# A hybrid encoder layer on one core: VectorE's rows taken in twos, half of the one-hots on ScalarE, shorter norms, and another order of GELUs and gate loads

## What is computed

```python
q = (xt @ w_pq).reshape(T, 8, 256)
s1 = einsum('thd,nd->thn', q[..., :128], sub_keys1)     # 128 keys each
s2 = einsum('thd,nd->thn', q[..., 128:], sub_keys2)
v1, i1 = top_k(s1, 16); v2, i2 = top_k(s2, 16)
cand_s = (v1[..., :, None] + v2[..., None, :])          # 256 pairs
cand_i = (i1[..., :, None] * 128 + i2[..., None, :])
top_s, pos = top_k(cand_s, 16)
idx, gate = cand_i at pos, softmax(top_s)               # 8 heads x 16 experts per token
act = gelu(einsum('thkd,td->thk', peer_u[idx], x)) * gate
out = einsum('thk,thkd->td', act, peer_v[idx])
x = layer_norm(ALPHA * x + out)
```

## Time and profile before

| | us |
|---|---|
| median of 3 runs (lowest, highest) | 3692.41 (3690.04, 3693.42) |
| the profiled execution, whole | 3718.29 |
| its span in the trace | 3716.4 |
| PE busy in the span | 3221.2 (87%) |
| DVE busy | 2060.8 (55%) |
| POOL busy | 782.7 (21%) |
| ACT busy | 374.4 (10%) |

### The profile page before, as it was taken

One profiled execution on the slowest core, in us unless ns is written; L12 is line 12 of the kernel. 1 busy time (PEld: TensorE's weight loads), 2 busy tenths in 40 slices (PEclk: granted clock), 3 DMA queues, 4 the chain that ended last, 5 costly groups with the idle time before them and its releaser, 6 DMA issues.

```text
span 3716.4 us, 27290 instructions
## 1 busy us (share of the span) xinstructions
PE 3221.2 (87%) x10446; PEld 1944.9 (52%) x10446; DVE 2060.8 (55%) x2868; ACT 374.4 (10%) x653; POOL 782.7 (21%) x546
## 2 busy tenths in 40 slices
PE   7998988899997597995555799959899997999995
PEld 4443433334445376774445444658544885448742
DVE  5356023232646767776777767555555554556564
ACT  1233012220102101110111000000000000000000
POOL 0000000000011102223222222343333433233230
PEclk9999998999998798997777899979999998999998
DMA  6221210037885567997777898998989999899992
GB/s 237 68 76 59 90 55 31 23 141 267 304 306 214 213 247 276 373 373 290 294 287 285 338 386 336 397 404 353 405 354 404 392 389 383 348 420 401 390 399 98
DMA packets 160817, 1031.76 MB, mean 278 GB/s; under 512 B 16448, under 2 KB 32960, under 8 KB 43328
## 3 DMA queue, kind: packets, MB, share of 16 engines
q0 software_dynamic: 75520, 547.39, 36.7%
q1 hardware_dynamic: 85184, 482.83, 33.8%
HBM read 1009.18 MB, written 20.97 MB: 277 GB/s over the span
## 4 chain that ended last, share of the span: by engine, by line
PE 50%; DVE 20%; DMA 20%; issue 5%; POOL 2%; ACT 1%; SPq 0%; DVEq 0%; ACTq 0%
PE ps L1032 15%; DMA arena<-peer_u,arena 12%; PE ps L1005 10%; PE ps L646 9%; DVE arena L1656 5%; PE ps L804 3%; DMA arena<-peer_ut 3%; DVE arena L1645 2%; PE ps L894 2%; DMA arena<-peer_v,arena 2%; POOL arena L579 2%; DVE arena L1683 2%; DMA arena<-peer_vt 2%; DVE arena L1585 1%; DVE arena L1582 1%
## 5 line engine op out<-in xcount | busy, mean ns | idle before, releaser
L1005 PE MATMUL ps<-arena 128*128 128x256 f32 x4096 | 896.3, 382 | 52.5 <-DMA arena<-peer_ut 52.5
L1032 PE MATMUL ps<-arena 128*128 128x512 f32 x2048 | 890.1, 598 | 49.5 <-DMA arena<-peer_vt 26.5
L1645 DVE CUSTOM_DVE_ANT_0 arena<-arena 128x2048 f32<-128x2048 f32 x256 | 586.3, 2290 | 559.3 <-DMA arena<-peer_u,arena 558.9
L1005 PEld LDWEIGHTS ps<-arena 128*128 128x128 f32 x4096 | 783.1, 192 | 162.4 <-issue 54.0
L1032 PEld LDWEIGHTS ps<-arena 128*128 128x128 f32 x2048 | 393.2, 192 | 544.2 <-issue 519.8
L579 POOL DMA_INDIRECT arena<-peer_v,arena x256 | 398.9, 1558 | 1126.6 <-DVE arena L1656 1096.5
L1656 DVE SCALAR_TENSOR_TENSOR arena<-arena 128x2048 f32<-128x2048 f32 x256 | 601.4, 2349 | 49.1 <-DMA arena<-peer_v,arena 44.2
L568 POOL DMA_INDIRECT arena<-peer_u,arena x256 | 368.2, 1438 | 925.6 <-DVE arena L1645 679.0
L646 PE MATMUL ps<-arena 128*128 128x512 f32 x832 | 363.3, 599 | 12.0 <-ACT arena L1111 11.0
L646 PEld LDWEIGHTS ps<-arena 128*128 128x128 f32 x832 | 160.0, 193 | 213.7 <-issue 213.7
L1069 ACT ACTIVATE arena<-ps 128x512 f32<-128x512 f32 (+4 forms) x247 | 146.7, 611 | 1030.1 <-PE ps L1017 224.7
(11 more groups left out here) (174 smaller groups left out, 1962.2 us busy)
## 6 DMA issues: line engine op xcount, KB each, us to landing
arena<-peer_ut SPq DMA_DIRECT2D x128, 1024.0 KB, 9.6
arena<-peer_vt SPq DMA_DIRECT2D x128, 1024.0 KB, 9.1
arena<-w_row SPq DMA_DIRECT2D x52, 1024.0 KB, 4.9
arena<-w_mix SPq DMA_DIRECT2D x48, 1024.0 KB, 4.8
arena<-w_once SPq DMA_DIRECT2D x76, 512.0 KB, 3.5
arena<-w_feat SPq DMA_DIRECT2D x20, 1024.0 KB, 4.8
dense_gates<-arena SPq DMA_DIRECT2D x8, 2048.0 KB, 6.7
arena<-dense_gates SPq DMA_DIRECT2D x16, 1024.0 KB, 18.8
```

The costliest lines, as they stand in the source:

```text
L1005: last = pe.matmul(ps[:, (e // 2) % 4, (e % 2) * DT:(e % 2 + 1) * DT], w[:, kt * P:(kt + 1) * P], XTD[:, kt * DT:(kt + 1) * DT], start=(kt ...
L1032: last = pe.matmul(bank(4 + (c % 2) * 2 + tb), G[:, t * DT + tb * P:t * DT + (tb + 1) * P], w[:, i * 512:(i + 1) * 512], start=(t == 0), s ...
L1645: dve.tensor_tensor_reduce(UB[e], UB[e], xrow(b), 1.0, 0.0, ALU.mult, ALU.add, DOT[r // 4 % 2][:, r % 4:r % 4 + 1]).then_inc(u_free, 1)
```

## The change

- **Rows.** `row_step` becomes `row(k)`: dot of row k+4, then add of row k. `some_rows(n)` does the next n rows. Before the tail VectorE takes rows in twos, mostly between the two halves of a routing, which is split into `best_keys` and `best_pairs`, and after it. 90 rows come before V0 instead of 84; in the tail they are spread in halves of a step (`half_pos`). The second V buffer opens at row 13 instead of 9.
- **One-hots.** VectorE makes only the gated one, with four `tensor_scalar` of 128x128 for each step; ScalarE makes the other with four Abs of 128x128 (the distance of the iota from the number) and one Relu of 128x512 (1 - distance). TensorE waits for both. They come in 16 groups of four steps before U tiles 17 to 32, with two rows of VectorE's within each group.
- **Routings of block 1.** Their products move to after U tiles 2, 5, 8, 11, the transposition to after tile 15. Two of the four routings come before V0, the other two at positions 8 and 15.
- **Norms.** Two passes in place of three. In the last dense group the statistics of blocks 2 and 3 are taken column group by column group, block 1's norm stands ahead of the last `add_dense`, and the last two blocks share one reciprocal square root.
- **ScalarE.** `gelu_rows` and `gate_exps` stand elsewhere between the evictions; `d_turned("x2T")` comes ahead of the GELU it followed.
- **Gates.** In groups 1 to 3 `load_gates` comes later in SyncE's queue, and `weigh` comes at positions 12 and 18 of a U phase and early in the V phase instead of after every eighth position.

```diff
-PQ_AFTER = [3, 7, 11, 15]
-TURN_AFTER = 21
-ONEHOT_BEFORE = [24 + 2 * k for k in range(DT // TG)]
+PQ_AFTER = [2, 5, 8, 11]
+TURN_AFTER = 15
+ONEHOT_FROM = 17
-ROWS_BEFORE = 21
-ROUTE_POS = [2, 12, 19, 26]
+HALVES_BEFORE = 45
+ROUTE_POS = {8: 2, 15: 3}
-V1_FROM = 9
+V1_FROM = 13
 (SyncE)
-                    for i in range(TILES[g] // 8):
-                        q = FIRST[g] // 8 + i
-                        if g and q + 2 < NK // 8 and p == start + 8 * i + 7 + SLOTS:
-                            load_gates(q + 2)
+                    q, n = FIRST[g] // 8, TILES[g] // 8
+                    if g and p == start + TILES[g] - 4:
+                        load_gates(q + 2)
+                    if g and n > 3 and p == start + TILES[g] - 2:
+                        load_gates(q + 3)
+                    if 0 < g < 3 and p == start + TILES[g] + 20:
+                        load_gates(q + n)
+                        load_gates(q + n + 1)
 (TensorE)
-                    pe.wait_ge(oh_ready, n + 1)
+                    pe.wait_ge(first_hot, n + 1)
+                    pe.wait_ge(second_hot, n + 1)
 (ScalarE)
+            def second_one_hots(n):
+                if n >= 2:
+                    act.wait_ge(oh_mm, n - 1)
+                hot = OH[n % 2][:, 4 * NK:8 * NK]
+                for k in range(4):
+                    t = DT + 4 * n + k
+                    last = act.activation(hot[:, k * NK:(k + 1) * NK], IOTA, ACT.Abs, bias=TB[:, t:t + 1])
+                last.then_inc(hot_dist, 1)
+                act.wait_ge(hot_dist, n + 1)
+                act.activation(hot, hot, ACT.Relu, bias=ONES[:, 0:1], scale=-1.0).then_inc(second_hot, 1)
+            for n in range(DT // 4):
+                if n % 8 == 0 and n:
+                    gelu_rows()
+                second_one_hots(n)
+                if n:
+                    stage_gates(n - 1)
+                if n % 8 == 5:
+                    gelu_dense(0, t)
+                    t += 2
 (VectorE)
-                link(dve.tensor_scalar(dst, src, MV[:, 0:1], RSTD, ALU.subtract, ALU.mult))
-                link(dve.tensor_tensor(dst, dst, gain, ALU.mult))
-                return dve.tensor_tensor(dst, dst, bias, ALU.add)
+                link(dve.scalar_tensor_tensor(out=dst, in0=src, scalar=MV[:, 0:1], in1=gain, op0=ALU.subtract, op1=ALU.mult))
+                return dve.scalar_tensor_tensor(out=dst, in0=dst, scalar=RSTD, in1=bias, op0=ALU.mult, op1=ALU.add)
+            def row(k):
+                j, part = divmod(k, 4)
+                if part == 0:
+                    dve.wait_ge(gel_done, j + 1)
...
+                if j + 1 < RSTEPS:
+                    dot(k + 4)
+                if part == 0:
+                    dve.wait_ge(act_done, j + 1)
+                add_row(k)
+            def first_one_hots(n):
+                if n >= 2:
+                    dve.wait_ge(oh_mm, n - 1)
+                for k in range(4):
+                    t = 4 * n + k
+                    last = dve.tensor_scalar(OH[n % 2][:, k * NK:(k + 1) * NK], IOTA, TB[:, t:t + 1],
+                                             TB[:, 2 * DT + t:2 * DT + t + 1], ALU.is_equal, ALU.mult)
+                last.then_inc(first_hot, 1)
+            def d_route(n, between):
+                b, c = 2 + n % 2, n // 2 - 2
+                best_keys(n, f"d.key{c}.{n % 2}")
+                some_rows(between)
+                best_pairs(b, c)
...
                 for k, b in enumerate((3, 1)):
                     add_mix(b, c, (c % 2) * 2 + k, f"mix31.{c}")
-                if c == 0:
-                    row_step(0)
-                if c == 1:
-                    gates(1, 0, 1)
-                if c == 2:
-                    row_step(1)
+                if c < 2:
+                    some_rows(4)
             first_norm(3, "mix3.3")
...
-            for n in range(8, 12):
-                route(n, 2 + n % 2, n // 2 - 2, f"d.key{n // 2 - 2}.{n % 2}")
-                if n < 11:
-                    row_step(n)
-                gates(n, 2 + n % 2, n // 2 - 2)
-            row_step(11)
+            for n in range(6, 12):
+                d_route(n, 2)
+                some_rows(2)
+                d_gates(n)
             dve.wait_ge(tb_ev, 1)
-            for k in range(DT // TG):
-                row_step(12 + k)
-                for n in range(8 * k, 8 * k + 8):
-                    one_hot(n)
-            row_step(12 + DT // TG)
+            for n in range(DT // 4):
+                first_one_hots(n)
+                if n % 4 == 1:
+                    some_rows(2)
+            best_keys(12, "b1.key0")
+            best_pairs(1, 0)
+            some_rows(2)
+            gates(12, 1, 0)
+            best_keys(13, "b1.key1")
+            best_pairs(1, 1)
...
+                    if g == 3 and c == 3:
+                        rows_until(POSITIONS)
+                        dve.wait_ge(v_free, 2 * HK)
+                        norm(ACC1, ACC1, GAIN3_G, GAIN3_B, dve_tick).then_inc(y_ready, 1)
                     add_dense(g, c)
+                    if g == 3:
+                        last = last_stats(c)
...
+            rsqrt(RSTD3, var, NEWTON3)
+            for tb in range(DB):
+                xr = xrow(2 + tb)
+                link(dve.scalar_tensor_tensor(out=xr, in0=xr, scalar=MV3[:, 2 * tb:2 * tb + 1], in1=GAIN3_G,
+                                              op0=ALU.subtract, op1=ALU.mult))
+                dve.scalar_tensor_tensor(out=xr, in0=xr, scalar=RSTD3[:, tb:tb + 1], in1=GAIN3_B,
+                                         op0=ALU.mult, op1=ALU.add).then_inc(y_ready, 1)
```

More of the change, by code:

```diff
@@ L1367, in rows_until @@
+            stage_gates(n)
+            gelu_rows()
+            for t in range(t, TILES[0], 2):
+                gelu_dense(0, t)
+                if t == ONEHOT_FROM + DT // 16 - 1:
+                    gate_exps(12)
+            gate_exps(13)
+            assert steps[0] == ROWS_BEFORE, steps
             def rows_until(p):
-                while nxt[0] < RSTEPS and ROW_POS[nxt[0]] <= p + ROW_LEAD:
-                    gelu_rows(nxt[0])
-                    nxt[0] += 1
+                while steps[0] < RSTEPS and half_pos(2 * steps[0] - 1) <= p:
+                    gelu_rows()
@@ L1385, in _ @@
             rows_until(POSITIONS)
-            assert order == ACT_STEPS and nxt[0] == RSTEPS
+            assert order == ACT_STEPS and steps[0] == RSTEPS
         @block.vector
@@ L1680, in one_hot, with some_rows @@
+            def some_rows(n):
+                for k in range(rows[0], rows[0] + n):
+                    row(k)
+                rows[0] += n
+            def first_one_hots(n):
                 if n >= 2:
                     dve.wait_ge(oh_mm, n - 1)
-                turn = TB.rearrange("p (a t) -> p a t", a=3)
-                link(dve.tensor_tensor(oh, IOTA.unsqueeze(1).unsqueeze(1).broadcast_to([P, 2, 4, NK]),
-                                       turn[:, 0:2, here].unsqueeze(3).broadcast_to([P, 2, 4, NK]), ALU.is_equal))
@@ L1722, in _ @@
             gates(0, 0, 0)
-            for s in range(4):
-                dot(s)
-            route(1, 0, 1, "b0.key1")
+            dot(0)
+            dot(1)
+            best_keys(1, "b0.key1")
+            dot(2)
+            dot(3)
+            best_pairs(0, 1)
+            some_rows(2)
+            gates(1, 0, 1)
             for c in QUAD:
```

260 lines of the change are left out of this document (140 added, 120 removed).

## The result

| | before | after |
|---|---|---|
| median (lowest, highest), 4 runs each in one session | 3692.91 (3690.04, 3698.17) | 3501.57 (3494.50, 3503.96) |
| ratio to before, 95% interval | | 0.9477 [0.9459, 0.9495] |
| the profiled execution, whole | 3718.29 | 3503.96 |
| its span | 3716.4 | 3502.0 |

The account below looks back on a forecast made before the run. Bound: VectorE's rows and routings to V0, then PE with a few transfers, then VectorE. V0 at 1986, tail 1545 and end 19.5 gave span 3551, whole 3553, less 25.9: median 3527 us, range 3470 to 3605.

Parts of the forecast that it names:

- 1. The early norms: Four norms in a row at the start, each 1.2 us shorter with two passes: -5 us.
- 2. Mix to U tile 0: Rows in twos and an earlier GELU close PE's gaps; U tile 0 starts 35 us earlier, norms included, at 1433.
- 2. To gates 11: Rows in twos up to the twelfth gates: 540 us of VectorE work, 118 of waiting, ending near 1643.
- the good end of 1595: Twelfth gates' end with 70 us of VectorE waiting; part of the all-good-ends rival, 3480 us, chance 0.12.
- the slower rival: Early rows: a gather's round stays before each row, gain gone from 9.9 us a row; near 3757, chance 0.05.
- the account of the prediction: Early rows: time to gates 11 less first dot and 271 us, over 56 rows: 6.9 us a row.
- 3. The one-hots: Sixteen periods of 17.5 us before U tiles 17 to 32, 280 us in all; V0 at 1986.
- the rival of switching tables: One-hots: ScalarE's Abs and Relu in different sets, 2.6 us more a step: +56, 3583 us, chance 0.02.
- 4. The tail: V0 to last quad: PE's 1505.1 us stay, gaps fall from 83.6 to 40: 1545 us, to 3531.
- what is late next is DMA: Tail: once the late `weigh` is cured, DMA must move 591 MB, 393 GB/s over 1505 us.
- The rival in which DMA stays at 375 GB/s: DMA is the bound: tail +31 us, stretch before the one-hots +14; 3572 us, chance 0.16.
- 5. The end: After the last quad: add, statistics, root, four passes and output take 19.5 us instead of 40.7.

Follow-up runs that it names:

- e1: The changed kernel with three passes in each norm and the three last norms at the very end as before; 3539.70 us, 0.9570.
- e2: The changed kernel with both one-hots made by VectorE, eight `tensor_scalar` a step, and none by ScalarE; 3499.83 us, 0.9443.
- e8: The kernel before, with only the order changed: dot of row k + 4 right before add of row k; 3656.97 us, 0.9903.
- e9: The changed kernel with both one-hots made by VectorE in the old form, two `tensor_tensor` a step, groups kept; 3500.42 us, 0.9462.
- e5: The changed kernel with gate loads and weighing of groups 1 to 3 in their old places; 3459.30 us, 0.9333.

## Why the prediction was right, and where not

**What bounds it** held: VectorE's rows and routings to V0, then PE with transfers, then VectorE.

**1. The early norms.** 5 us were forecast to the mix and 13.4 came. With the old norms (e1) the mix starts at 802.3, as in before, but e2, which has the new ones, has 798.1, and after 789.0. In the timelines of PE the loop's first eight matmuls of L770 start at 617.79, where before had theirs (L756) at 622.91: 5 us, as forecast, are there by then. The other 8 come within the attention loop, where the clock differs (last section). That they are no effect of the change is borne out by e8, which has the old norms and starts the mix at 788.9.

**2. Mix to U tile 0.** Forecast 30 us of gain from the mix on (35 with the norms); 55.9 came. What was mis-sized is the list of gaps: I priced the 8.0 and the 23.2, and PE had four more over 10 us in the same stretch of the timeline of before:

```profile
1125.99 3.67 PE L814 MATMUL ps<-arena 128*128 128x128 f32 x16 [10.77 <-DVE arena L1551]
...
1227.34 16.27 PE L931 MATMUL ps<-arena 128*128 128x512 f32 x32 [11.66 <-DVE arena L1557]
...
1416.90 3.79 PE L944 MATMUL ps<-arena 128*128 128x128 f32 x16 [12.57 <-ACT arena L1069]
1433.58 3.50 PE L814 MATMUL ps<-arena 128*128 128x128 f32 x16 [12.90 <-ACT arena L1069]
```

They come to 47.9 us. In after PE is idle 50.3 us from the mix to U tile 0 in place of 102.5. The gap before 1137.7 did close, as said, but another of 4.3 opened before it.

**2. To gates 11.** Forecast 1643, measured 1589, which is beyond even the good end of 1595. Of the 54 us, 31 are waits of VectorE (87 in place of 118, by the view above with its smaller rows), 9 an earlier start (the first dot came at 976.4, not 985, and 8 of that are the clock's), and 15 its work, which I put at 540 us and which was 612.6 - 87.3 = 525. The 172 us of waiting that I took for the old stretch were too few as well: its waits add up to 202. The row's round was forecast too short: the chain of waits of after has one row from 1026.53 to the next add at 1037.20, 10.7 us and not 8.1:

```profile
1026.53 2.36 DVE arena L1723
1028.89 0.26 issue
1029.15 8.03 DMA arena<-peer_v,arena
```

V needs 8.03 us to land, where I took 5.45. I had read that row as issued alone, and it was not; in the timeline of POOL in before U is issued 1.25 us behind it:

```profile
1062.11 0.94 POOL L568 DMA_INDIRECT arena<-peer_u,arena  x1 [0.30 <-issue]
```

So U behind V does not explain the difference. What differs is how full DMA was meanwhile: a share of 0.78 at 266 GB/s in before's 5.4 us, of 0.98 at 381 GB/s in after's 8.0. In the nine rounds from 1006.14 to 1095.97, with one V buffer, a row took 10.0 us, forecast 8.1; that is over the 9.9 us from which the slower rival decided. But over all 56 rows, with the first dot where it was, the account of the prediction gives (1589 - 976 - 271) / 56 = 6.1 us a row, where the forecast had 6.9 and the rival needed 9.9. PE's wait at the turn was 16.25 us, not 33. From U tile 0 to the turn I had put 84 MB, counting all rows of the last six rounds; 190.5 us at 394 GB/s are 75 MB, since some of these rows came before U tile 0. With a DMA share of 0.97 little more was to be had there.

**3. The one-hots.** 16 periods took 269.5 us, 16.8 each, where 17.5 was forecast, PE was busy 74% of them, and turn to V0 took 334.8 where 343 was forecast: right by the number, but the credit given to the second engine was wrong. The 17.5 stood between 13.8 us of VectorE's rows and round trips and 15.7 us of gathers, with VectorE's share of a step at 0.6 to 1.1 us in place of 1.9. e2 and e9 show that this saving carries nothing: with all of it back on VectorE the period is the same. The row for it was there: one-hots of eight steps took 15.3 us, so four steps and two rows in the *old* form are 7.65 + 9.3 = 16.9 us, below my 17.5. I had priced the new form against the old period and never the old form in the new groups. The parts of the price were right, as the groups of ScalarE in after, 1589 to 1930 us, show:

```profile
L1295 ACT ACTIVATE arena<-arena 128x128 f32<-128x128 f32 x256 | 81.0, 390 | 0.0
L1298 ACT ACTIVATE arena<-arena 128x512 f32<-128x512 f32 x64 | 46.2, 722 | 2.1
```

A step costs ScalarE 81.0 / 64 + 46.2 / 64 + 0.58 for the staging copy = 2.6 us (2.4 was taken). No table load stands at either line: the rival of switching tables is out, and the trace agrees with the Trainium skill ("ScalarE: Activation LUTs", Table sets), which has both functions in every set.

**4. The tail.** 40 us of gaps were forecast, 59.8 measured: this step failed. SyncE's wait behind `weigh` went as said, to zero. But the new places were not needed for it, since e5 with the old ones has 23.5 us of such waits in pieces of at most 2.6. Most likely the wait of 36.7 went because VectorE was done with its rows sooner: in e8, which has nothing of the change but the order of dots and adds, the longest such wait is 11.1 us, and PE's gap of 38.1 is one of 13.8. What came in its place is the collision of gate loads with bursts of gathers: 57.7 of the 59.8 us lie in the four largest gaps, 41.2 of them behind the two pairs in V phases. It was named as "what is late next is DMA", and priced by a mean rate over the tail; the loss sits in some 40 us around each pair. The rival in which DMA stays at 375 GB/s seems borne out by the 373 of after, but e5 moves the same rows and pieces at 384: the rate followed the gaps and did not set them.

**5. The end.** 19.5 forecast, 19.6 measured.

**The offset.** The forecast of the profiled execution was 3553 and it took 3504, 49 us off; the median was 25 off. I took 25.9 us from the profile to the median as in before; after's profiled execution lies 2.4 above its median. The steps up to V0 came out 62 us shorter than forecast and the tail 13.5 longer; that the median is only 25 off is in part luck, since nothing told me that the profiled execution of before lay so much further above its median than the next one would, and half of the error in the steps was cancelled by this.

## What to carry to other kernels

Price each part of a change against the old form *in the new arrangement*, not against the old period: here the arrangement (order of dot and add, halves of a routing with two rows between) carried the gain up to V0, and the second engine none. Before work goes to an engine with room, look at what that engine waits for: ScalarE stood behind the stores. Two consumers of one strictly ordered queue of gathers should take the buffers in the order in which they are issued. When a wait in a load queue goes, look for what the moved load now stands beside: behind a megabyte of gate loads at a moment of full DMA PE stood up to 9 us, behind two of them up to 26, and VectorE's waits at a barrier tell where its gathers will burst.

## What the runs showed of the hardware

TensorE's clock in the attention loop differs between executions that do the same work there. The timeline of PE in after, then the second of the two rows in e9:

```profile
617.79 3.70 PE L770 MATMUL ps<-arena 128*128 128x512 f32 x8 [1.69 <-ACT arena L1084]
...
629.75 5.40 PE L770 MATMUL ps<-arena 128*128 128x512 f32 x8 [0.69 <-ACT arena L1084]
```

```profile
630.24 3.70 PE L770 MATMUL ps<-arena 128*128 128x512 f32 x8 [0.69 <-ACT arena L1083]
```

The granted clock was 1.00 in the first of these stretches, the level of 2.4 GHz, and 0.68 in the second, so partly that of 1.2; e9 took 3.70 us for the same matmuls, as for the first eight. In both kernels PE did the same small matmuls before them, with the same pauses of 1.0, 0.2 and 0.7 us. The loop's stretch of after, then that of e1, whose work there is the same but for its norms:

```profile
560.00:789.00 229.00, 200.90 (x495) 78.86 (x494) 68.56 (x163) 67.44 (x136) 8.52 (x15) 0.95 0.10 37
```

```profile
560.00:802.00 242.00, 213.98 (x507) 84.18 (x506) 68.55 (x163) 67.45 (x136) 8.54 (x15) 0.92 0.09 35
```

5 of the 13 us between them are the norms; the other 8 go with the granted clock, 0.95 against 0.92. The mix starts between 783 and 798 in the kernels with the new norms, and at 788.9 to 802.4 in those with the old ones. Whoever compares profiles of such kernels should align them at the mix first.

A gather's issue on GpSimd took longer beside VectorE's dots and adds of 128x2048, and not beside its one-hots. In the one-hots of after the issues that began while a dot or an add ran took 1.9 to 2.8 us and ended 0.8 to 0.9 us behind that operation; those that lay wholly beside `tensor_scalar` took 0.94 to 0.98, against 0.93 with VectorE idle. In e9 the issues at 1655.87 and 1672.73, beside `tensor_tensor` of 512 and 1024 columns, took 0.93 and 0.94, so a second input alone does not do it; whether the kind of operation or its length does, no run separates. It cost little in the one-hots of after: VectorE waited 5.9 us in all for gathers.
